# Softmax weights divided before the turns instead of the outputs after them: one change to a four-layer fp32 kernel

## What is computed

```
s = q @ k.T * scale + bias          # 128 x n
p = exp(s - max(s)) ; p = p / sum(p)  # the sum takes in the sink, where there is one
y = p @ v                           # 128 x 64
```

## Times and profile before

| | us |
|---|---|
| median of 3 runs (2631.64 to 2635.26) | 2632.3 |
| the profiled execution's own time | 2634.5 |
| its span | 2632.7 |
| PE busy in the span | 2554.5 (97%) |
| ACT busy | 966.0 (37%) |
| DVE busy | 928.2 (35%) |
| POOL busy | 1220.9 (46%) |
| mean granted clock of PE | 0.99 |

### The profile page before, as it was taken

One profiled execution on the slowest core, in us unless ns is written; L12 is line 12 of the kernel. 1 busy time (PEld: TensorE's weight loads), 2 busy tenths in 40 slices (PEclk: granted clock), 3 DMA queues, 4 the chain that ended last, 5 costly groups with the idle time before them and its releaser, 6 DMA issues.

```text
span 2632.7 us, 46466 instructions
## 1 busy us (share of the span) xinstructions
PE 2554.5 (97%) x16163; PEld 2202.8 (84%) x16163; DVE 928.2 (35%) x1715; ACT 966.0 (37%) x2245; POOL 1220.9 (46%) x1033
## 2 busy tenths in 40 slices
PE   6999999999998999999999899999999999999999
PEld 6767888888866888888999788999999967998897
DVE  4263221222143321125663353440442254441341
ACT  4384222232177422224333233331333486322221
POOL 5454444444474544444343454443444355444443
PEclk9999999999999999999999899999999999999999
DMA  5212222222231223222221002222222201222222
GB/s 170 84 34 88 91 99 89 96 101 83 89 72 31 96 94 104 81 96 104 84 81 68 1 1 72 88 97 86 89 100 77 80 2 42 95 90 102 88 94 98
DMA packets 80489, 212.94 MB, mean 81 GB/s; under 512 B 30336, under 2 KB 33024, under 8 KB 80384
## 3 DMA queue, kind: packets, MB, share of 16 engines
q1 hardware_dynamic: 80384, 211.56, 23.8%
HBM read 209.44 MB, written 2.10 MB: 80 GB/s over the span
## 4 chain that ended last, share of the span: by engine, by line
PE 89%; issue 4%; ACT 3%; POOL 2%; DVE 1%; POOLq 0%; DMA 0%; ACTq 0%; DVEq 0%; SPq 0%
PE ps L1149 79%; PE ps L1395 3%; PE ps L1277 1%; PE ps L1307 1%; PE ps L1290 1%; ACT s_sb L863 1%; POOL w_lo L540 1%; ACT p_t L875 1%; PE ps L1311 0%; POOL bias_sb L622 0%; PE ps L1226 0%; DVE s_sb L1574 0%; PE ps L1387 0%; PE ps L1181 0%; POOL h_lo L639 0%
## 5 line engine op out<-in xcount | busy, mean ns | idle before, releaser
L540 POOL TENSOR_TENSOR w_lo<-raw,w_hi 128x512 fp32r<-128x512 f32 (+1 forms) x704 | 976.2, 1409 | 1168.7 <-ACT w_hi L764 1168.5
L764 ACT ACTIVATE w_hi<-raw 128x512 fp32r<-128x512 f32 (+1 forms) x704 | 426.5, 653 | 1348.5 <-PE ps L1149 1336.0
L1149 PE MATMUL ps<-h_hi,w_hi 128*128 128x264 f32 (+2 forms) x3216 | 903.3, 330 | 2.0 <-DVE padded L1549 1.1
L1149 PE MATMUL ps<-h_lo,w_hi 128*128 128x264 f32 (+2 forms) x3216 | 896.5, 328 | 0.0
L1149 PE MATMUL ps<-h_hi,w_lo 128*128 128x264 f32 (+2 forms) x3216 | 895.7, 328 | 0.0
L1149 PEld LDWEIGHTS ps<-h_hi,w_hi 128*128 128x128 f32 x3216 | 543.0, 189 | 63.0 <-issue 2.7
L1149 PEld LDWEIGHTS ps<-h_lo,w_hi 128*128 128x128 f32 x3216 | 542.7, 189 | 57.2 <-issue 1.0
L1149 PEld LDWEIGHTS ps<-h_hi,w_lo 128*128 128x128 f32 x3216 | 541.5, 189 | 55.3
L1149 PE MATMUL ps<-act_hi,w_lo 128*128 128x512 f32 (+1 forms) x880 | 280.9, 352 | 0.0
L1149 PE MATMUL ps<-act_hi,w_hi 128*128 128x512 f32 (+1 forms) x880 | 280.2, 351 | 0.0
L1149 PE MATMUL ps<-act_lo,w_hi 128*128 128x512 f32 (+1 forms) x880 | 279.3, 350 | 0.0
(11 more groups left out here) (219 smaller groups left out, 2274.8 us busy)
## 6 DMA issues: line engine op xcount, KB each, us to landing
raw<-slabs_d SPq DMA_DIRECT2D x288, 512.0 KB, 3.2
raw<-slabs_d SPq DMA_DIRECT2D x64, 704.0 KB, 4.0
rpb_raw<-rpb_d SPq DMA_DIRECT2D x24, 224.0 KB, 4.0
bias_sb<-alibi_d SPq DMA_DIRECT2D x6, 384.0 KB, 3.8
x<-x_d SPq DMA_DIRECT2D x1, 2048.0 KB, 12.6
out_d<-x SPq DMA_DIRECT2D x8, 256.0 KB, 4.6
mem_in<-mem_d SPq DMA_DIRECT2D x1, 1024.0 KB, 8.8
dn_cst<-dn_consts_d SPq DMA_DIRECT2D x1, 512.0 KB, 5.1
```

The lines of the kernel that those rows point to most:

```text
L540: nc.gpsimd.tensor_tensor(w_lo[:, s, a * P:b * P], raw[:, s, a * P:b * P], w_hi[:, s, a * P:b * P].bitcast(f32), ALU.subtract).then_inc(lo ...
L764: nc.scalar.activation(w_hi[:, s, a * P:b * P], raw[:, s, a * P:b * P], ACT.Copy)\
L1149: last = nc.tensor.matmul(ps[:, s * 2 * BANK + po:s * 2 * BANK + po + n], w[:, s, wk], a[:, k, to:to + n], start=(k == 0 and w is w_hi and ...
```

## The change

1. `invert(p)` on DVE: behind the reciprocal it waits for it and multiplies the exponentials of both heads, in place in `s_sb`, by the reciprocal of their sum (two `tensor_scalar`, 128 x n, a per-partition scalar). `turn` on PE waits for these (`p_scaled`) and no longer for the exponentials (`p_ready`).
2. The output in PSUM is then finished. The transpose at L1311, `spread`, `move_y`, the tiles `p_rec` and `y_sb` and their semaphores are gone. ACT's `y_hi(p-2)` rounds from PSUM into `h_hi`; DVE's `normalise(p-3)` makes `h_lo = PSUM - h_hi`; POOL has no `y_lo` left.
3. POOL's chores for `rpb`: query staging; key staging and the mask of h = 0; the mask of h = 1; value staging. DVE waits for each head's mask by itself.
4. The two attentions of layers 0 and 1 are joined: `Pair.back` reaches into the prior stage, and the closing steps of the first are left out.
5. Start: slab 2 is loaded ahead of the five small inputs, slab 3 ahead of the first ALiBi tile; `x` has its own semaphore; in `memkv` PE runs slab 1 before the sum of squares.

```diff
@@ Pair
             def back(self, k):
-                n = 2 * len(self.st.blocks)
-                return Pair(self.st, self.g, self.pos - k) if self.pos >= k else Pair(self.st, self.g - 1, self.pos - k + n)
+                n, prior = 2 * len(self.st.blocks), self.st.prior
+                if self.pos >= k:
+                    return Pair(self.st, self.g, self.pos - k)
+                if prior and isinstance(self.g, int) and self.g == 0:
+                    return Pair(prior, prior.nt // 2 - 1, self.pos - k + 2 * len(prior.blocks))
+                return Pair(self.st, self.g - 1, self.pos - k + n)
@@ sync
-            sp.dma_start(x[:, :, META:TOK], d["x"].rearrange("(m p) t -> p m t", p=P)).then_inc(loaded, 16)
+            sp.dma_start(x[:, :, META:TOK], d["x"].rearrange("(m p) t -> p m t", p=P)).then_inc(x_loaded, 16)
+
+            def load_slabs(q, s, size, src, at):
+
+                sp.wait_ge(lo_done, 2 * (2 * q + s - 1))
+                sp.dma_start(raw[:, s, 0:size * P], src[at]).then_inc(raw_full[s], 16)
+
+            load_slabs(1, 0, UP, d["slabs8"], 2)
             sp.dma_start(x[:, :, 0:META], d["meta"].rearrange("(m p) t -> p m t", p=P)).then_inc(loaded, 16)
...
+            load_slabs(1, 1, UP, d["slabs8"], 3)
@@ gpsimd prepare
-                return [stage_q, stage_k, stage_v, mask]
+                def mask(i, h):
+
+                    if h == 0:
+                        pool.wait_ge(rpb_full, i * 64 + 64)
+                        if not isinstance(i, int) or (i - 1) * nb + st.pair0 >= 1:
+                            pool.wait_ge(max_ready, 2 * ((i - 1) * nb + st.pair0))
+                    nc.gpsimd.tensor_tensor(
+                        bias_sb[:, i % 2, h, :].rearrange("p (r c) -> p r c", c=GRID), rpb_raw[:, h, :, ::-1],
+                        grid_mask.unsqueeze(1).to_broadcast([P, RPB_R - 1, GRID]), ALU.add).then_inc(rpb_masked, 1)
+
+                def k_and_mask(i):
+                    stage_k(i)
+                    mask(i, 0)
+
+                def second_mask(i):
+                    mask(i, 1)
+
+                if st.bias == "rpb":
+                    return [stage_q, k_and_mask, second_mask, stage_v]
+                return [stage_q, stage_k, stage_v]
@@ scalar attend
+                def y_hi(p):
                     act.wait_ge(pv_done, p.count + 1)
-                    if counted(p.count - 1):
-                        act.wait_ge(y_lo_ready, p.count - 1)
-                    nc.scalar.activation(y_sb[st.h][:, p.slot, 0:p.nq], bank(6 + p.slot)[:, 0:p.nq], ACT.Copy)\
-                        .then_inc(y_moved, 1)
-
-                def y_hi(p):
-                    act.wait_ge(y_ready, p.count + 1)
-                    nc.scalar.activation(h_hi[st.h][:, st.y + p.tile, p.q], y_sb[st.h][:, p.slot, 0:p.nq],
+                    nc.scalar.activation(h_hi[st.h][:, p.st.y + p.tile, p.q], bank(6 + p.slot)[:, 0:p.nq],
                                          ACT.Copy).then_inc(y_hi_ready, 1)
...
-                    if p.back(1).exists:
-                        spread(p.back(1))
                     if p.back(2).exists:
-                        move_y(p.back(2))
-                    if p.back(3).exists:
-                        y_hi(p.back(3))
+                        y_hi(p.back(2))
                 over_pairs(act.Fori, st, step)
+                if st.joined:
+                    return
@@ tensor memkv
-                        first_pair(st, 0, mem_hi, mem_lo)
+                        slab(q, 0, 0, mem_hi, mem_lo, made=h_ready, at=DT * st.pre.n)
+                        slab(q, 1, 0, mem_hi, mem_lo)
+                        sum_squares(st.pre)
@@ tensor attend
-                        pe.wait_ge(p_ready, u + 1)
+                        pe.wait_ge(p_scaled, u + 1)
...
-                        pe.wait_ge(y_ready, p.count - 1)
+                        pe.wait_ge(y_lo_ready, p.count - 1)
...
-                    pe.wait_ge(rec_ready, p.count + 1)
-                    nc.tensor.transpose(out[:, P:P + p.nq],
-                                        p_rec[0:p.nq, p.slot, :],
-                                        ident[0:p.nq, 0:p.nq]).then_inc(pv_done, 1)
+                            last = nc.tensor.matmul(out[HD * h:HD * h + HD, 0:p.nq],
+                                                    v_st[0:n, p.tile_slot, vb, HD * h:HD * h + HD],
+                                                    p_t[0:n, p.slot, h, j, 0:p.nq], start=(j == 0),
+                                                    stop=(j == len(cs) - 1))
+                    last.then_inc(pv_done, 1)
@@ vector attend
-                    if p.b == 0 and st.bias == "rpb":
-                        wait(rpb_masked, 2 * p.tile + 2)
...
+                        if p.b == 0 and st.bias == "rpb":
+                            wait(rpb_masked, 2 * p.tile + h + 1)
...
                 def invert(p):
                     wait(p_ready, 2 * p.count + 2)
-                    if counted(p.count - 1):
-                        wait(rec_ready, p.count - 1)
+                    if counted(2 * p.count - 2):
+                        wait(p_scaled, 2 * p.count - 2)
                     recip(p_inv[0:p.nq, p.slot, :], p_sum[0:p.nq, p.slot, :]).then_inc(inv_ready, 1)
+                    wait(inv_ready, p.count + 1)
+                    for h in range(2):
+                        s_h = s_sb[0:p.nq, p.slot, h, 1:1 + p.n]
+                        ts(s_h, s_h, p_inv[0:p.nq, p.slot, h:h + 1], None, ALU.mult).then_inc(p_scaled, 1)
                 def normalise(p):
-                    wait(y_moved, p.count + 1)
-                    y = y_sb[st.h][:, p.slot, 0:p.nq]
-                    tt(y, y, bank(6 + p.slot)[:, P:P + p.nq], ALU.mult).then_inc(y_ready, 1)
+                    wait(y_hi_ready, p.count + 1)
+                    tt(h_lo[st.h][:, p.st.y + p.tile, p.q], bank(6 + p.slot)[:, 0:p.nq],
+                       h_hi[st.h][:, p.st.y + p.tile, p.q].bitcast(f32), ALU.subtract).then_inc(y_lo_ready, 1)
```

More of the change, by code:

```diff
@@ L61, in __init__ @@
         self.queries = None
+        self.prior, self.joined = None, False
         self.gate = self.used = blk
@@ L98, in att @@
     def att(**kw):
+        before = out[-1]
         s = add("att", **kw)
+        if before.kind == "att":
+            s.prior, before.joined = before, True
         c["pair"] += kw["nt"] * len(kw["blocks"])
@@ L286, in build @@
         p_inv = small("p_inv", [P, 2, 2])
-        p_rec = small("p_rec", [P, 2, P])
         q_hi, q_lo = (small(n, [P, 2, TOK], f32r) for n in ("q_hi", "q_lo"))
@@ L346, in quad @@
             return ps[:, k * BANK:k * BANK + DN_H * n].rearrange("p (h n) -> p h n", h=DN_H)
-        mem_loaded, cst_loaded, loaded = sem("mem_loaded"), sem("cst_loaded"), sem("loaded")
+        mem_loaded, cst_loaded, x_loaded, loaded = (sem(n) for n in ("mem_loaded", "cst_loaded", "x_loaded", "loaded"))
         raw_full = [sem(f"raw_full{s}") for s in range(RING)]
@@ L357, in build @@
             sem(n) for n in ("hi_staged", "qk_staged", "v_staged", "s_done", "max_ready", "p_ready"))
-        pt_done, pv_done, inv_ready, rec_ready = (sem(n) for n in ("pt_done", "pv_done", "inv_ready", "rec_ready"))
+        pt_done, pv_done, inv_ready, p_scaled = (sem(n) for n in ("pt_done", "pv_done", "inv_ready", "p_scaled"))
         pt_ready = [sem(f"pt_ready{h}") for h in range(2)]
-        y_moved, y_ready, y_hi_ready, y_lo_ready = (sem(n) for n in ("y_moved", "y_ready", "y_hi_ready", "y_lo_ready"))
+        y_hi_ready, y_lo_ready = sem("y_hi_ready"), sem("y_lo_ready")
         alibi_full, rpb_full, rpb_masked = sem("alibi_full"), sem("rpb_full"), sem("rpb_masked")
@@ L372, in build @@
         stored = sem("stored")
-        N_FIRST, N_LOADS = 2, 6
+        N_FIRST, N_LOADS = 2, 5
         META_T, SEQ_T = slice(0, META), slice(META, TOK)
@@ L468, in _ @@
             sp.dma_start(w_ba[:, :, :], d["w_ba"].rearrange("(m p) t -> p m t", p=P)).then_inc(loaded, 16)
[L470 to L475, removed]
+            load_slabs(1, 1, UP, d["slabs8"], 3)
+            at, seen = 2 * RING, {UP: 2 * RING, DOWN: 0}
             def stream(upto):
@@ L632, in attend @@
                 nb = len(st.blocks)
[L634 to L641, removed]
                 chores = prepare(st)
@@ L649, in attend @@
                             pool.wait_ge(acc_free[s], (st.slab0 - 2) // 2)
-                    chores[0](0)
-                    chores[1](0)
-                    chores[3](0)
+                    for chore in chores[:-1]:
+                        chore(0)
                     pool.wait_ge(val_kept, st.val0)
-                    chores[2](0)
+                    chores[-1](0)
                 def tile(i, chores, tile0):
                     for b in range(nb):
-                        if b < 4 and chores:
+                        if b < len(chores):
                             chores[b](tile0)
[L661 to L664, removed]
                 tile(1, chores, 1)
@@ L679, in attend @@
```

(15 more changed lines are left out.)

15 lines of the change are left out of this document (3 added, 12 removed).

## The result

The changed kernel took 2775.7 us (median of 4 runs, 2775.2 to 2780.9) against 2632.8 (2631.6 to 2635.3; one more run than in the table above): ratio 1.055, 95% interval 1.053 to 1.056. I had forecast +61 us, with a range that ended at 2730; it was +143. The profiled execution has a span of 2773.9, 141.2 more than before, and the three attention stretches (first scores of a stretch to the first product of the output) are together 143.5 longer.

A forecast was written before the change was run, and what follows sets the result against it. PE was taken as the bound, ACT's loop right behind in rpb; 19.0 + 20.8 + 21.3 + 3 + 12 - 8.2 + 0.8 - 5.4 - 2.0 = +61.3 us, forecast 2694 us, range 2662 to 2730.

The forecast's parts named there:

- ALiBi pairs: 24 pairs, DVE's scores, reciprocal, scales and the turn in a row: 3.23 us a pair against 2.365, +20.8 us.
- rpb pairs: 24 pairs, reciprocal, self-wait, scale and hand-over ahead of the turn: 0.79 us a pair, none covered, +19.0 us.
- masks: POOL's masks ahead of rpb scores come in time, so PE's waits shrink: -5.4 us, bounds -6.4 and -4.
- band pairs: 40 pairs, scores, reciprocal, scales and turn in a row: 2.84 us a pair against 2.307, +21.3 us.
- the loops: Attention pairs: the turn waits for DVE's reciprocal and scale, making ALiBi 3.23, rpb 3.99 and band 2.84 us a pair.
- alternation: Band: ACT's loop is about as long as DVE's, and two alternating limits give more than either: +3 us.
- joins: Joined attentions of layers 0 and 1: drain goes, closing grows, gain 4.1 us each, -8.2 us in all.
- Rival A: All attention pairs: the scale is hidden and PE alone sets the pair, so the kernel gets faster, 2583 us; 6%.
- POOL beside the scales: DVE's scales in the attentions may wait while POOL runs, 0.2 us each: +12 us, bounds 0 and 40.
- rival B: Attention pairs: both scales wait whenever POOL runs, 28 us more than forecast, 2722 us; 20%.
- C: Attention pairs: PE's clock falls to 1.2 GHz and PE sets the pairs, 38 us more, 2730 us; 8%.
- the memory pairs: Seven pairs in each joined attention, with the scale path in place of scores: 2.76 us a pair against 2.64.

The follow-up runs named there:

- e11: Changed kernel with one more PE product of 512 columns ahead of the first head's turn, in the band pairs only: 2779.4 us, ratio 1.056.
- e7: Kernel before with only the new masks, joined attentions and order of loads at the start, output normalised late as before: 2618.9 us, ratio 0.994.
- e8: Kernel before with the joined attentions alone, output normalised late as before: 2626.3 us, ratio 0.997.
- e3: Changed kernel with each DVE scale also writing its sum to a spare column, another form of tensor_scalar: 2752.5 us, ratio 1.045.
- e4: Changed kernel with one more PE product of 256 columns ahead of each head's turn, to keep PE awake: 2759.9 us, ratio 1.047.
- e12: e9 with one more PE product of 512 columns ahead of the first head's turn, in the band pairs only: 2722.3 us, ratio 1.034.
- e9: Changed kernel with the two scales moved from DVE to ACT, DVE keeping the reciprocal: 2744.7 us, ratio 1.042.

## Why the prediction was right in kind and wrong in size

| part | forecast | trace after less before |
|---|---|---|
| start (to the first scores) | -2.0 | -4.7 |
| ALiBi pairs (last least value less first) | +20.8 | +34.5 |
| rpb pairs, masks | +19.0 - 5.4 | +37.3 |
| from there to the output's product, layers 0 and 1 | -8.2 | +3.5, +4.6 |
| band pairs | +21.3 + 3 | +59.7 |
| close of the band | +0.8 | +3.9 |
| POOL | +12 | within the above |
| rest | 0 | +2.4 |
| sum | +61.3 | +141.2 |

- **Right: the loops, though drawn somewhat short.** The turn waits for DVE (the releaser in the rows above), and the steps of the loop are those of the prediction. Pairs that met neither POOL nor the slow clock last 3.41 to 3.46 us in ALiBi (once 3.66), 4.01 to 4.10 in rpb and at most 3.21 in the band (e11's five pairs above, which hold the added product), against 3.23, 3.99 and 2.84: some 5, 1 and 12 us over 24, 24 and 40 pairs, the band's 3 for alternation taken off. A scale was 0.06 to 0.08 us dearer than I drew from the earlier trace rows, the self-wait cheaper (0.09, not 0.15). Masks (-5.7 for -5.4) and joins as such (-7.0 for -8.2) were right by e7 and e8. The start's row of the table proves nothing, as e8's first scores moved by 2.4 us without it. Rival A is out.
- **Failed: "POOL beside the scales", taken as 12 of 0 to 40.** 43 us of waits were there. Their mean, 43 / 208 = 0.21 us, is the 0.2 of the prediction; wrong was to count them in part only. The two scales of 4.36 us made a pair of 7.5 us where one without a wait took 4.0, so h = 1 had no slack either. The argument against rival B (one SBUF input only) was the wrong way round: the earlier trace rows showed a block of 1.23 us, and no row that I read showed an instruction of that kind passing POOL. The page SBUF — State Buffer of the Trainium skill, section "Who interferes with whom", says that `tensor_scalar` can run in a mode that shares a port pair with GpSimd, in which the second to issue is blocked, and that the form that also writes out its accumulator is not among these; the traces of the changed kernel (4.36 us for two) and of e3 (0.75 each beside the same masks) agree on both.
- **Failed: B and C as cases that exclude each other and my forecast.** They came together. PE's share of the stretches fell (in layer 0 from 77.34 of 84.55 us to 92.69 of 122.59) and its clock with it, which lengthens the turn that stands in the loop; with added products it came back (0.97 and 1.00 in e4, 1.00 in e12's band). I had ruled it out by PE at full clock with 2.41 of 4.00 us busy; that row is from another stage and didn't carry over. My own figures added up, 61 + 28 (B) + 38 (C) = 127, would have been near. By stage, C had 4 (ALiBi), 21 (rpb) and 13 (band). Pairs alike but for the clock give these estimates: ALiBi 0.3 to 0.5 us in the pairs at half clock, some 4; band 2.1 a tile, 7 x 2.1 = 15; in rpb, 24 pairs took 119.6 us, which less 24 x 4.04 and 18.6 of waits leaves 4. So C's 38 was near the measured size in part by luck, its rpb term being far too large. No run changes the clock alone over a whole stretch of the changed kernel; e12 does so for e9's band.
- **Right by itself, and lost to the two above: the memory pairs, 2.76 us.** Two of layer 0's, one at either clock, from reciprocal to reciprocal:

```profile
209.31:212.06 2.75, 2.30 (x22) 1.45 (x22) 1.86 (x5) 1.88 (x8) 0.00 (x0) 1.00 0.03 6
...
225.52:228.80 3.28, 3.10 (x18) 2.15 (x18) 1.86 (x6) 1.76 (x8) 0.00 (x0) 0.50 0.00 0
```

At full clock a pair lasts what I forecast. Two further pairs met POOL (3.93 and 3.49), and behind them the clock fell to half, so that the mean is 3.3 us, against 2.7 in e7. In layer 0 the way from DVE's last ALiBi scores to the output's product is 33.4 us, 25.9 in e7, and the joins' gain became a loss.

What adds up, as an estimate: my sum without its POOL term is 49; loops drawn short 18; waits for POOL at their length 43; the clock 4 + 4 + 15 and, in the eight memory pairs at half clock, 8 x 0.53 = 4. That is 137 of the 141 us. The measured sizes of 43 for a term taken as 12 and of about 27 for one taken as 0 are what put the result out of my range. The split between POOL and the clock isn't exact, as each changes the other: the clock falls behind a long wait, and e3's 23 us hold some of both.

## What to carry to other kernels

Before an instruction is put between two engines that hand work back and forth, write the loop out for every kind of pair, the short ones too, and look at what the helper engine runs at that moment: a wait on such a loop costs its whole length, and the pairs behind it can be slow as well (here 4.4 to 5.4 us behind an rpb pair of 7.5, where 4.0 is usual). When a forecast lengthens a loop around PE, price the lower clock inside the forecast, not as a rival beside it. And one change of several parts can hold gains that a bad part hides: without the early normalisation this one is 0.6% faster.

## What the runs showed of the hardware

- A `tensor_scalar` from SBUF to SBUF waited for POOL's running instruction to end (2.14 us beside a mask of 2.16, once 5.03 behind four in a row); with a sum written beside it, it passed POOL (0.75 us at most in all 208) but took 0.75 us instead of 0.49 at 512 columns, and 0.08 more for the reading.
- A fp32 product with a diagonal matrix has twice the records of the transpose of the same tile.
- ACT's copy with a scale within SBUF took 0.50 us at 256 columns, DVE's scale 0.35.
- At a granted clock of 0.50 a pair of these loops took 0.3 to 0.9 us more than at 1.00 (3.94 against 3.46 us, 3.28 against 2.75, 3.95 against 3.10).
